# Embedding gate by seven half-size products, with two regular up-projection blocks ahead of them and one operand difference made by GpSimd

## The reference, cut to what matters

```python
f_gate, f_up = jnp.split(x @ w_ffn_in, 2, axis=-1)      # 2 x 2816 columns
ffn = (jax.nn.silu(f_gate) * f_up) @ w_ffn_out
ple = jax.nn.sigmoid(x @ w_ple_gate) * (p_i @ w_ple_proj)   # 1024 columns
return layer_norm(ALPHA * x + ffn + ple, ln2_g, ln2_b)
```

## Time and profile before

| what | us |
|---|---|
| median of three runs | 1786.07 (1785.73 to 1786.78) |
| the profiled execution | 1786.35 |
| its span, first to last instruction | 1784.6 |
| PE busy in it | 1762.5 |
| granted TensorE clock, mean | 0.998 |

### The profile page before, as it was taken

How to read it: one execution, slowest core, us unless ns; L and a number is a source line. 1 busy time by engine, 2 the same in 40 slices (tenths; PEclk the granted TensorE clock), 3 DMA queues, 4 the chain that set the end, 5 groups by cost and what they waited for, 6 DMA issues and landing times.

```text
span 1784.6 us, 28654 instructions
## 1 busy us (share of the span) xinstructions
PE 1762.5 (99%) x9966; PEld 1538.7 (86%) x9966; DVE 1248.9 (70%) x2413; ACT 944.4 (53%) x1841; POOL 850.6 (48%) x458
## 2 busy tenths in 40 slices
PE   9999999999999999999999999999999999999997
PEld 9888888878779999988898888888787799999886
DVE  6379988867778888513363899887778788884133
ACT  4544777844455555422244557787444565654222
POOL 5446943344443434354434578434443444444542
PEclk9999999999999999999999999999999999999999
DMA  5332211223333333233333321112232333332431
GB/s 192 99 94 92 60 60 60 63 73 102 95 118 95 110 105 103 88 118 107 95 99 102 98 83 60 60 60 64 80 105 94 107 107 97 117 96 83 130 98 68
DMA packets 47077, 166.62 MB, mean 93 GB/s; under 512 B 5472, under 2 KB 5728, under 8 KB 46944
## 3 DMA queue, kind: packets, MB, share of 16 engines
q1 hardware_dynamic: 46080, 163.60, 29.6%
q10 hardware_dynamic: 864, 1.28, 0.2%
HBM read 162.76 MB, written 2.10 MB: 92 GB/s over the span
## 4 chain that ended last, share of the span: by engine, by line
PE 78%; issue 9%; POOL 5%; DVE 5%; ACT 2%; DMA 0%; POOLq 0%; DVEq 0%; SPq 0%; ACTq 0%
PE banks L1133 20%; PE banks L1135 20%; PE banks L1134 20%; POOL sb_wl L604 5%; PE banks L1184 4%; PE banks L1185 4%; PE banks L1186 4%; PE banks L1240 2%; PE banks L1287 2%; DVE banks L1682 1%; PE banks L1271 1%; DVE sb_hconv L1977 1%; PE banks L1216 1%; PE banks L1270 0%; POOL sb_csq_sum L635 0%
## 5 line engine op out<-in xcount | busy, mean ns | idle before, releaser
L604 POOL TENSOR_TENSOR sb_wl<-sb_wraw,sb_wh 128x1024 fp32r<-128x1024 f32 x223 | 547.5, 2459 | 657.1 <-ACT sb_wh L732 637.4
L1133 PE MATMUL banks<-sb_xh,sb_wh 128*128 128x512 f32 (+1 forms) x1184 | 428.6, 362 | 3.9 <-POOL sb_wl L604 2.9
L1135 PE MATMUL banks<-sb_xh,sb_wl 128*128 128x512 f32 (+1 forms) x1184 | 411.9, 348 | 0.0
L1134 PE MATMUL banks<-sb_xl,sb_wh 128*128 128x512 f32 (+1 forms) x1184 | 411.2, 347 | 0.0
L732 ACT ACTIVATE sb_wh<-sb_wraw 128x1024 fp32r<-128x1024 f32 x215 | 227.1, 1057 | 300.4 <-PE banks L1135 184.1
L1133 PEld LDWEIGHTS banks<-sb_xh,sb_wh 128*128 128x128 f32 x1184 | 224.9, 190 | 30.8 <-issue 5.1
L1135 PEld LDWEIGHTS banks<-sb_xh,sb_wl 128*128 128x128 f32 x1184 | 224.3, 189 | 29.3
L1134 PEld LDWEIGHTS banks<-sb_xl,sb_wh 128*128 128x128 f32 x1184 | 225.2, 190 | 18.3
L1134 PE MATMUL banks<-sb_t_lo,sb_wh 128*128 128x256 f32 x640 | 181.1, 283 | 0.0
L1133 PE MATMUL banks<-sb_t_hi,sb_wh 128*128 128x256 f32 x640 | 181.1, 283 | 0.0
L1135 PE MATMUL banks<-sb_t_hi,sb_wl 128*128 128x256 f32 x640 | 181.1, 283 | 0.0
(11 more groups left out here) (345 smaller groups left out, 3952.2 us busy)
## 6 DMA issues: line engine op xcount, KB each, us to landing
sb_wraw<-in_weights SPq DMA_DIRECT2D x264, 512.0 KB, 3.5
sb_wraw2a<-in_weights SPq DMA_DIRECT2D x20, 512.0 KB, 3.5
sb_wraw2b<-in_weights SPq DMA_DIRECT2D x20, 512.0 KB, 4.5
sb_u<-in_x SPq DMA_DIRECT2D x8, 256.0 KB, 6.4
out<-sb_u SPq DMA_DIRECT2D x8, 256.0 KB, 2.1
sb_praw<-in_ple ACTq DMA_DIRECT2D x2, 512.0 KB, 4.3
sb_par<-in_params ACTq DMA_DIRECT2D x2, 98.5 KB, 2.6
sb_rope_tmp<-in_freq ACTq DMA_DIRECT2D x1, 24.0 KB, 4.5
```

The source lines that it names most:

```text
L604: nc.gpsimd.tensor_tensor(wl[:, slot(t), :], wraw[:, t % 2, :], wh[:, slot(t), :].bitcast(F32), ALU.subtract).then_inc(lo_ready, 1)
L1133: nc.tensor.matmul(out, wh_, xh_, start=start, stop=False, skip_group_check=onto)
L1134: nc.tensor.matmul(out, wh_, xl_, start=False, stop=False, skip_group_check=onto)
L1135: return nc.tensor.matmul(out, wl_, xh_, start=False, stop=stop, skip_group_check=onto)
```

## The change

The numbers of tiles and of matmuls in the regular way stay at two pairs, but these are now pairs of FFN blocks 0 and 1 and stand first (T_R); the eight gate blocks become four pairs (NG) ahead of the 20 FFN pairs in the list of Winograd pairs, so that there are 24 (NS). The four gate pairs have their own forms of c21, c22, tanh, product and sum into `u`, on 128x512 instead of 128x256. The bias of the norm is added within the combinations (T3, T2, T4, four 128x256 operations each, on DVE), so that they need not wait for ACT's pass over `u`; that pass moves to places 1.6 to 5.8. The fourth combination, the difference of the token halves (T1), has no bias and is made by POOL, as is its low part. The two regular blocks' nonlinear part ("gate", "hidden") is put in the same lists. At the end, the last unit runs inside the down-projection, behind its first tile. DVE has one more operation of 128x4 at the start of a layer (`bias_step`).

```diff
-T_PG = T_PP + 4
-T_FI = T_PG + DK
-T_FO = T_FI + 2 * FK
+T_R = T_PP + 4
+NR, NG = 2, DK // 2
+NS = NG + FK - NR
+T_S = T_R + 2 * NR
+T_FO = T_S + 2 * NS
...
-A_BANK, E_BANK, B_BANK, G_BANK, S1_BANK, S2_BANK, S4_BANK = (0, 1), 4, 2, 3, 5, 6, 7
-TAIL_BANKS = ((5, 6), (7, 4))
+A_BANK, E_BANK, B_BANK, G_BANK, S1_BANK, S2_BANK, S4_BANK = (0, 1), 2, 3, 4, 5, 6, 7
+R_BANKS = ((2, 3), (1, 4))
+T3, T2, T4, T1 = 1, 2, 3, 0
+T_MADE = {T3: 4, T2: 8, T4: 12}
+T_ORDER = (T3, T2, T4)
...
-    act, dve, pool = [], [(-6, ("sum3", 0)), (-4.6, ("sum1", 0))], []
+    act = [(-9, ("t high", T3)), (-8.9, ("gate", 0)), (-8.8, ("t high", T2)), (-4.4, ("gate", 1)), (-1.4, ("t high", T4)),
+           (-5, ("t high", T1)), (10, ("hidden high", 0)), (17, ("hidden high", 1))]
+    act += [(1.6 + 0.6 * j, ("bias", j)) for j in range(DK)]
+    dve = [(-9, ("t", T3)), (-8.9, ("t", T2)), (-8.8, ("t low", T3)), (-8.7, ("t low", T2)), (-8.6, ("hidden", 0)),
+           (-6, ("sum3", 0)), (-4.6, ("sum1", 0)), (-2.4, ("t", T4)), (-0.2, ("t low", T4)),
+           (1.55, ("hidden", 1)), (11, ("hidden low", 0)), (18, ("hidden low", 1))]
+    pool = [(-9, ("t", T1)), (0.5, ("t low", T1))]
...
+        late = 1 if j < NG else 0
         act += [(at["a11"] + 1, ("m1", j)), (at["s3"] + 1, ("m7", j)), (at["s2"] + 1, ("u2", j)),
-                (at["a12"] + 2, ("th first", j)), (at["a22"] + 3, ("high first", j)), (at["s4"] + 1, ("th second", j)),
-                (at["s4"] + 3, ("high second", j))]
+                (at["a12"] + 2 + late, ("th first", j)), (at["s4"] + 1, ("th second", j))]
+        if j >= NG:
+            act += [(at["a22"] + 3, ("high first", j)), (at["s4"] + 3, ("high second", j))]
         dve += [(at["a12"] + 1, ("c11", j)), (at["a22"] + 1, ("c21", j)), (at["s1"] + 1, ("c22", j)),
-                (at["a22"] + 2, ("product first", j)), (at["a22"] + 4, ("low first", j)),
+                (at["a22"] + 2 + late, ("product first", j)), (at["a22"] + 4, ("low first", j)),
...
+                    if what == "t":
+                        pool.wait_ge(z_ready, layer * 16 + DK)
+                        nc.gpsimd.tensor_tensor(t_raw[:, T1], u[:, 0:KH, 0:HALF], u[:, 0:KH, HALF:S],
+                                                ALU.subtract).then_inc(t1_made, 1)
+                        continue
+                    if what == "t low":
+                        pool.wait_ge(t1_high, layer + 1)
+                        nc.gpsimd.tensor_tensor(t_lo[:, T1], t_raw[:, T1], t_hi[:, T1].bitcast(F32),
+                                                ALU.subtract).then_inc(t1_low, 1)
+                        continue
...
+                    elif what == "t high" and n == T1:
+                        act.wait_ge(t1_made, layer + 1)
+                        nc.scalar.activation(t_hi[:, n], t_raw[:, n], ACT.Copy).then_inc(t1_high, 1)
+                    elif what == "t high":
+                        act.wait_ge(t_made, layer * T_MADE[T4] + T_MADE[n])
+                        nc.scalar.activation(t_hi[:, n], t_raw[:, n], ACT.Copy,
+                                             scale=-1.0 if n in (T2, T4) else 1.0).then_inc(t_high, 1)
+                    elif what == "bias":
+                        act.wait_ge(x_ready, layer * 16 + (DK + n + 1))
+                        act.wait_ge(t_made, layer * T_MADE[T4] + T_MADE[T4])
+                        act.wait_ge(t1_made, layer + 1)
+                        nc.scalar.activation(u[:, n], u[:, n], ACT.Identity, bias=column("l1b", n)).then_inc(x_raw, 1)
+                    elif what == "gate":
+                        gate(T_R + 2 * n, first, R_BANKS[n][0], th[:, n, :], 0.0, ffn_th)
...
+                    elif what == "th first" and n < NG:
+                        act.wait_ge(c11_ready, at + (n + 1))
+                        act.wait_ge(c21_ready, at + (n + 1))
...
-                for k in range(0, DK, 2):
-                    if k == 2:
-                        pe.wait_ge(pp_out, layer * DK + DK)
-                    if k == 6:
-                        pe.wait_ge(h_done, layer * (DK + FK) + (2 + 2))
-                    side_by_side(T_PG + k, PG_BANK[k], xh, xl, x_block if k == 0 else lambda kk: None)
+                side_by_side(T_R, R_BANKS[0][0], xh, xl, x_block)
+                pe.wait_ge(pp_out, layer * DK + DK)
+                for c in range(2):
+                    project(T_R + 2 + c, first, xh, xl, DK, [R_BANKS[1][c]])
...
+                    if j == 0 and source == "t":
+                        if k0 == T1:
+                            pe.wait_ge(t1_low, layer + 1)
+                        else:
+                            pe.wait_ge(t_low, layer * 3 + (T_ORDER.index(k0) + 1))
+                    if kind == "a11" and j == 1:
+                        pe.wait_ge(ffn_s, layer * NR + NR)
+                    elif kind == "a11" and j >= NG + 2:
+                        pe.wait_ge(h_done, layer * FK + (NR + j - 2 - NG + 1))
+                    elif kind == "a11" and j >= 2:
+                        pe.wait_ge(gated, layer * NG + (j - 1))
...
+                    if j < 2:
+                        pe.wait_ge((c21_ready, c11_ready)[j], layer * NS + NS)
                     for part in range(PARTS):
-                        pe.wait_ge(h_done, layer * (DK + FK) + (DK + min(DK * (part + 1), FK) + 2))
+                        pe.wait_ge(h_done, layer * FK + min(DK * (part + 1), FK))
                         down(T_FO + PARTS * j + part, part, first, 2 + j % 2, part == 0, part == PARTS - 1)
+                        if j == 0 and part == 0:
+                            unit(NU - 1)
...
-                b11, b12, b21, b22 = [u[:, k:k + KH, half] for k in (0, KH) for half in (first_half, last_half)]
-                made = layer * 4
-                dve.wait_ge(x_raw, layer * DK + DK)
-                v.tensor_tensor(t_raw[:, 0], b11, b12, ALU.subtract).then_inc(t_made, 1)
-                v.tensor_tensor(t_raw[:, 1], b22, b12, ALU.subtract).then_inc(t_made, 1)
-                dve.wait_ge(t_made, made + 2)
-                v.tensor_tensor(t_raw[:, 2], b11, t_raw[:, 1], ALU.add).then_inc(t_made, 1)
-                dve.wait_ge(t_made, made + 3)
-                v.tensor_tensor(t_raw[:, 3], b21, t_raw[:, 2], ALU.subtract).then_inc(t_made, 1)
...
+                    elif what == "t" and n == T3:
+                        for k in range(KH):
+                            v.scalar_tensor_tensor(t_raw[:, T3, k], u[:, KH + k, last_half], bias_step[:, k:k + 1],
+                                                   u[:, k, last_half], ALU.add, ALU.subtract).then_inc(t_made, 1)
+                    elif what == "t" and n == T2:
+                        dve.wait_ge(t_made, made + T_MADE[T3])
+                        for k in range(KH):
+                            v.scalar_tensor_tensor(t_raw[:, T2, k], u[:, k, first_half], column("l1b", k),
+                                                   t_raw[:, T3, k], ALU.add, ALU.add).then_inc(t_made, 1)
+                    elif what == "t" and n == T4:
+                        dve.wait_ge(t_made, made + T_MADE[T2])
+                        for k in range(KH):
+                            v.scalar_tensor_tensor(t_raw[:, T4, k], u[:, KH + k, first_half], column("l1b", KH + k),
+                                                   t_raw[:, T2, k], ALU.add, ALU.subtract).then_inc(t_made, 1)
+                    elif what == "t low":
+                        dve.wait_ge(t_high, layer * 3 + (T_ORDER.index(n) + 1))
+                        if n == T3:
+                            ins = v.tensor_tensor(t_lo[:, n], t_raw[:, n], t_hi[:, n].bitcast(F32), ALU.subtract)
+                        else:
+                            ins = v.scalar_tensor_tensor(t_lo[:, n], t_raw[:, n], -1.0, t_hi[:, n].bitcast(F32),
+                                                         ALU.mult, ALU.subtract)
+                        ins.then_inc(t_low, 1)
+                    elif what == "hidden":
+                        tc = th[:, n, :]
+                        dve.wait_ge(ffn_th, layer * NR + (n + 1))
+                        steps.done(v.scalar_tensor_tensor(tc, tc, 1.0, psum[:, R_BANKS[n][0], :], ALU.add, ALU.mult))
+                        steps.wait()
+                        dve.wait_ge(tile_used, first + (T_R + 2 * n + 2 + START))
+                        v.tensor_tensor(tc, tc, psum[:, R_BANKS[n][1], :], ALU.mult).then_inc(ffn_s, 1)
...
+                        if n < NG:
+                            v.scalar_tensor_tensor(psum[:, G_BANK, HALF:S], psum[:, E_BANK, 0:HALF], -1.0, u2[:],
+                                                   ALU.mult, ALU.subtract).then_inc(c21_ready, 1)
+                            return
...
+                    elif what in ("product first", "product second") and n < NG:
+                        c = int(what == "product second")
+                        g = psum[:, A_BANK[n % 2] if c else G_BANK, :].rearrange("p (b t) -> p b t", b=2)
```

(66 more changed lines are left out.)

190 lines of the change are left out of this document (73 added, 117 removed).

## The result

The changed kernel takes 1790.15 us (median of 11 runs, 1789.79 to 1791.83), the kernel before, in the same session, 1786.01 (11 runs, 1785.7 to 1786.78): a ratio of 1.0023, 95% interval [1.0015, 1.0031]. The forecast was 1788.3 in 1780 to 1794. The difference, 4.1 us, lies just over the 3.6 us that the prediction named as the bound of no change, in the case to which it gave 0.30. The profiled execution has a span of 1787.9 us.

The account below looks back on a forecast made before the run. PE was taken as the bound, busy 1762.5 of 1784.6 us. Per layer 5.9 us standstill against 4.81 gained gives +1.1, +2.2 in all: 1788.6 on the profiled 1786.35, 0.28 lower on the median, 1788.3; range 1780 to 1794.

Parts of the forecast that it names:

- the case to which it gave 0.30: Outcome slower than the kernel before by more than 0.2% (3.6 us); same had 0.48, faster 0.22.
- The gain on PE: PE's stage from first pair to down-projection: 257.64 falls to 252.83 us, 4.81 less per layer, if nothing new stands still.
- The mechanism: First Winograd pair's feeding: DVE operations with two SBUF inputs and POOL's reading SBUF block each other for the whole instruction.
- walk B: DVE's and POOL's lists, POOL slipping into DVE's runs whenever it can: 7.4 us standstill, +2.6 per layer net.
- the rows show both habits; I take 5.9: Standstill per layer taken between both walks' 4.9 and 7.4 us: +1.1 net per layer, +2.2 in all.
- walk A: DVE's and POOL's lists, DVE's runs kept whole while POOL waits: 4.9 us standstill, +0.1 per layer net.
- Rival 1: DVE and POOL blocking costs little, standstill under 3.0 us per layer: 1780.5 us at 2 us left; chance 0.25.
- Rival 2: DVE overrun in the gate pairs, up to 11.2 us per pair of 10.08: +7.4 us, 1793.5; chance 0.11.
- The mark that I had named for this rival: Rival 2 decides once DVE's busy share is at 100% through the second to fourth pair.
- Rival 3: Tail: c21 or the last low part delays the down-projection, 0.5 to 1.5 us per layer: 1790.5; chance 0.06.
- The marks: Signs for: stage 257.7 to 260.2 us, first-pair waits at s2, a12, s1, long T operations, none before or in tail.

Follow-up runs that it names:

- The last version: Banks version with the gate pairs' sum into u earlier on DVE and POOL's low part of T1 earlier: 1780.83 us, ratio 0.9966 to the kernel before.
- the two runs with less or no contention: Changed kernel with POOL's T1 and its low part cut to 8 of 1024 columns, 1784.13 us; and the banks version, 1782.24 us.
- where T3 was guarded: Changed kernel with POOL's low part of the last regular weight tile waiting until DVE has written T3: 1788.74 us, ratio 1.0014 to the kernel before.
- the banks version: Changed kernel with T3 and T2 in four free result banks instead of SBUF, four ACT copies more, T4 earlier: 1782.24 us, ratio 0.9978 to the kernel before.
- the run with another order: Gate pairs' sum into u moved earlier in DVE's order: 1788.19 us in the changed kernel, 1781.64 us in the banks version.
- m1 was put first: Changed kernel with ACT's copy m1 of the first pair ahead of the high part of T4: 1790.26 us, ratio 1.0022 to the kernel before.

## Why the prediction was nearly right

**The gain on PE, 4.81 us per layer: right.** No run contradicts 252.83 as the floor. The last version comes within 1.5 us of it in layer 0 and is 5.7 us faster than before; 2 x (4.8 - 1.5) = 6.6 would be due. The 1.0 us by which its span ends later behind layer 1 accounts for the missing 0.9.

**The mechanism: right.** T3's row and the two runs with less or no contention show it: 6 us less where POOL's operations shrink, 5 where the operands move. T3 ended at 508.75, where walk B had 509.5 on a clock 0.5 later.

**The size: the step "the rows show both habits; I take 5.9" is the one that failed.** It took a value between walk A (4.9) and walk B (7.4). The runs show B's habit each time that POOL became ready in a run of four such operations: it entered, in T3 of the changed kernel, in T2 where T3 was guarded. Walk A's example, 142.15 in the earlier trace rows, is also weaker than it looks: 3.85 is the row's length, not the wait. POOL's operation takes 2.4, so it waited 1.45 and let two of DVE's operations go first. Walk B's single terms against PE's measured delays:

| start | walk A | walk B | measured |
|---|---|---|---|
| s3, first pair | 0 | 1.0 | 0.9 |
| s2 | 1.6 | 1.8 | 2.1 |
| a12, a22 | 0.9 | 0.7 | 0.4 |
| s1 | 1.3 | 0.9 | 0.9 |
| second pair, first units | 0.4 | 1.0 | 0.8 |
| starts of third and fourth pair | 0.8 | 2.0 | 1.7 |

Every term lies within 0.3 of walk B's. The stage's own total is 6.7 against my 5.9: 0.8 per layer, 1.6 of the 1.85 us by which the forecast was low. B alone, +5.2, would have been 1.1 too high.

**Rival 1,** the blocking costs little: fallen. It describes the banks version, for which it would have been nearly right (1780.5 against 1782.2).

**Rival 2,** DVE overrun: its sign came in part, DVE busy 9.61, 9.96 and 9.97 of 10 in the second to fourth pair, but not its price, and the run with another order shows why. A DVE that stands for POOL is counted as busy, and one that is never waited for can be full without harm. The mark that I had named for this rival could not tell it from the forecast.

**Rival 3,** the tail: fallen. The down-projection's first stretch in the changed kernel, with the last unit inside it:

```profile
763.06:769.84 6.78, 6.78 (x37) 5.82 (x36) 1.19 (x3) 1.06 (x1) 2.39 (x1) 1.00 0.42 124
```

**The marks:** a stage of 257.7 to 260.2 (259.5), standstills at s2 for m1 and at s1, none before the first unit or in the tail: right. The standstill at a12, ended by POOL, did not come in the changed kernel (0.16; walk A had 0.9, walk B 0.3); it came at 1.17 only where m1 was put first. That s2 was "ended by ACT's copy" was right as a row and no cause. A clock under 1.00, named as a sign against it, did appear; it is told below.

## What to carry to other kernels

Where GpSimd's work is moved beside a run of DVE operations with both operands in SBUF, count its duration against DVE (2.14 of 2.40 us for each here), even if GpSimd is mostly idle; one operand in a free bank took the cost away. The engine that ends PE's wait is not the cause until moving its instruction shortens the sum of the waits: here 1.83 us at one place became 0.49 and 1.17 at two others. Work out late starts list by list, in order; where two readings of a contention give two sums, don't take a value between them: here one of the two, GpSimd getting in as soon as the running operation ends, fitted every late start within 0.3 us. And separate a row's length from its wait before a row is used as evidence.

## What was not expected of the hardware

**TensorE's clock fell after a 2 us standstill, in some places and not in others.** In layer 1 of the changed kernel PE stood still as in layer 0 (1.84 us before 1408.06), and then this window shows a granted clock of 0.50, the level of 1.2 GHz; the matmuls of 256 columns start 0.21 us apart there instead of 0.12:

```profile
1408.80:1412.10 3.30, 3.30 (x17) 3.30 (x17) 3.27 (x5) 3.02 (x7) 3.30 (x3) 0.50 0.37 137
```

In layer 0, behind the same standstill, it stayed at 1.00 (521.60 and on); where DVE made T1 it fell in layer 0 (523.6 to 526.8, 0.50) and not in layer 1, and in the changed kernel with the gate pairs' sum first in both layers. Of the ten stages with one standstill of 1.8 to 2.0 us, in five runs, it fell in four; in the others, with shorter ones, in none. The Trainium skill ("TensorE: Matmul & The Clock Gate", section "Part 1: The HAM clock gate (the "warmup" mystery)") says that idle time throttles the clock and that when it changes varies from run to run. The rows agree that idle time can bring the clock down, and they show it varying between two layers of one execution; they don't show what decides. It cost nothing here: both stages are of 259.5 us. The slower matmuls filled time in which PE would have waited for the next late unit.

**Who goes first is not settled by these runs.** POOL entered each run of four 128x256 operations in which it became ready, behind the one then running, but at 142.15 it waited 1.45 us and let two operations of 128x512 go first. The width alone doesn't keep it out, nor does the form `TENSOR_TENSOR`: in the banks version POOL, ready at 512.63, got in between two DVE operations of 128x512 that start 0.60 apart, and the second took 1.80 instead of 0.68.

```profile
512.63 0.68 DVE L2122 TENSOR_TENSOR sb_wl_raw<-sb_wraw 128x512 f32<-128x512 f32 x1
513.23 1.80 DVE L2127 TENSOR_TENSOR banks<-sb_wraw 128x512 f32<-128x512 f32 x1
...
512.63 1.84 POOL L708 TENSOR_TENSOR sb_wl<-sb_wraw,sb_wh 128x512 fp32r<-128x512 f32 x1 [3.09 <-ACT sb_wh L1052]
```

What kept POOL out at 142.15 was not tried.
